# Reordering the first stage of a fused decoder-layer kernel: norm sums ahead of and around the conditioning matmuls

## The reference, cut to what matters

```python
ada = jax.nn.silu(c) @ w_ada + b_ada
sh1, sc1, g1, shm, scm, gm, sh2, sc2, g2 = [a[:, None, :] for a in jnp.split(ada, N_ADA, axis=-1)]
h = modulate(rms_norm(x, ln1), sh1, sc1)
x = x + 0.5 * g1 * swiglu(h, w_f1_up, w_f1_down)
h = modulate(rms_norm(x, ln_mix), shm, scm)
...
x = x + gm * mix
h = modulate(rms_norm(x, ln2), sh2, sc2)
x = x + 0.5 * g2 * swiglu(h, w_f2_up, w_f2_down)
```

## Time and profile before

| | before |
|---|---|
| median of 3 runs | 2063.03 us |
| the profiled execution: its own time | 2063.94 us |
| its span (first to last instruction) | 2062.0 us |
| TensorE busy | 1956.5 us (95%) |
| VectorE / ScalarE / GpSimd busy | 1183.1 / 800.5 / 342.9 us |
| mean granted TensorE clock | 0.975 of full |
| first stage, up to the first `half_shift` | 58.90 us |
| start of the unbroken up matmuls | 92.86 us |

### The profile page before, as it was taken

How to read it: one execution, slowest core, us unless ns; L and a number is a source line. 1 busy time by engine, 2 the same in 40 slices (tenths; PEclk the granted TensorE clock), 3 DMA queues, 4 the chain that set the end, 5 groups by cost and what they waited for, 6 DMA issues and landing times.

```text
span 2062.0 us, 35562 instructions
## 1 busy us (share of the span) xinstructions
PE 1956.5 (95%) x13771; PEld 1887.8 (92%) x13771; DVE 1183.1 (57%) x1880; ACT 800.5 (39%) x1336; POOL 342.9 (17%) x319
## 2 busy tenths in 40 slices
PE   7599999999989999999999989699999999999997
PEld 5499999999979999989899878699999999999997
DVE  4865555555545354656756667755555555555554
ACT  3622232323234234355546554523222232444443
POOL 0222121222100001012103132312222121000000
PEclk9799999999999999999999999899999999999998
DMA  7022222222388675443343423122222222574743
GB/s 275 21 90 76 74 73 83 73 83 73 105 312 293 229 268 205 134 135 99 99 111 98 115 80 98 32 84 73 83 67 76 75 73 63 183 218 137 228 146 121
DMA packets 277621, 255.80 MB, mean 124 GB/s; under 512 B 11202, under 2 KB 222649, under 8 KB 277513
## 3 DMA queue, kind: packets, MB, share of 16 engines
q1 hardware_dynamic: 277357, 254.35, 38.8%
q10 hardware_dynamic: 164, 0.09, 0.0%
HBM read 224.08 MB, written 30.42 MB: 123 GB/s over the span
## 4 chain that ended last, share of the span: by engine, by line
PE 84%; DVE 7%; ACT 4%; DMA 2%; issue 2%; POOL 1%; SPq 0%; DVEq 0%; ACTq 0%; POOLq 0%
PE banks L631 44%; PE banks L667 24%; PE banks L576 9%; PE banks L582 1%; DVE mwl L1429 1%; PE banks L603 1%; DMA araw<-hidden 1%; ACT mwh L1157 1%; DVE y L390 1%; PE banks L587 1%; DVE xo L1434 0%; ACT xo L985 0%; PE banks L823 0%; DVE xT L1531 0%; PE banks L818 0%
## 5 line engine op out<-in xcount | busy, mean ns | idle before, releaser
L631 PE MATMUL banks<-xo,woh 128*128 128x272 f32 x4928 | 944.8, 291 | 38.0 <-DVE xo L1434 19.5
L631 PEld LDWEIGHTS banks<-xo,woh 128*128 128x128 f32 x4928 | 784.0, 191 | 40.5 <-issue 20.6
L631 PE MATMUL banks<-xo,wol 128*128 128x272 f32 x2464 | 718.5, 292 | 0.0
L667 PE MATMUL banks<-ahl,woh 128*128 128x384 f32 (+1 forms) x2112 | 518.7, 329 | 11.6 <-DVE wol L1591 11.4
L631 PEld LDWEIGHTS banks<-xo,wol 128*128 128x128 f32 x2464 | 469.2, 190 | 0.0
L667 PEld LDWEIGHTS banks<-ahl,woh 128*128 128x128 f32 x2112 | 371.6, 189 | 25.5 <-DVE wol L1591 14.8
L667 PE MATMUL banks<-ahl,wol 128*128 128x384 f32 (+1 forms) x1056 | 345.1, 327 | 0.0
L1450 DVE TENSOR_TENSOR pp<-pp,banks 128x544 f32<-128x544 f32 x220 | 154.7, 720 | 214.7 <-PE banks L631 214.7
L1591 DVE TENSOR_TENSOR wol<-ws,woh 128x512 fp32r<-128x512 f32 x264 | 183.3, 698 | 139.0 <-ACT woh L1102 137.9
L1102 ACT ACTIVATE woh<-ws 128x512 fp32r<-128x512 f32 x264 | 164.0, 624 | 166.9 <-PE banks L667 148.5
L576 PE MATMUL banks<-hh,mwh 128*128 128x384 f32 (+1 forms) x600 | 208.6, 348 | 15.3 <-DVE mwl L1429 11.3
(11 more groups left out here) (206 smaller groups left out, 1808.2 us busy)
## 6 DMA issues: line engine op xcount, KB each, us to landing
ws<-in_w_ffn_down SPq DMA_DIRECT2D x264, 256.0 KB, 3.3
ws<-in_w_ffn_up SPq DMA_DIRECT2D x88, 512.0 KB, 4.6
aiD<-in_w_ada SPq DMA_DIRECT2D x14, 2048.0 KB, 8.9
ws<-in_w_in SPq DMA_DIRECT2D x51, 512.0 KB, 3.8
hidden<-post SPq DMA_DIRECT2D x88, 272.0 KB, 2.6
araw<-hidden SPq DMA_DIRECT2D x88, 192.0 KB, 3.9
ws<-in_w_out SPq DMA_DIRECT2D x24, 512.0 KB, 3.7
ai<-in_w_ada SPq DMA_DIRECT2D x4, 2048.0 KB, 20.8
```

The source lines that it names most:

```text
L631: mm = pe.matmul(out, w[:, s, P * k:P * (k + 1)], x_operand(h, j, x)[:, k, :], start=(k == 0 and a == 0), stop=(k == 3 and a == 2))
L667: mm = pe.matmul(ps[4 * (p % 2) + m][:, 0:n], l[:, down_slot(s), P * m:P * (m + 1)], ahl[:, k, x, 0:n], start=(k == 0 and a == 0), stop=(k ...
```

## The change

On TensorE the wait for `csT` (`s_cs` at 2) goes from ahead of the square sums of half 0 to behind them, and the square sums of half 1 are cut in two, with the select of unit 0 between the parts. On ScalarE logarithm and exponential of half 0 come together ahead of those of half 1. On VectorE the slices of `half_scale` are spread in pairs between the unit's copies and stores, and `norm_factor(1)` goes from behind the copy of unit 1 to behind the store of unit 2.

```diff
@@ TensorE @@
-            pe.wait_ge(s_cs, 2)
             pe.wait_ge(s_ones, 1)
             pe.wait_ge(s_trev, 2 * NX)
-
             square_sums(0, 0, KT)
+            pe.wait_ge(s_cs, 2)
+
             for u in range(AU_FIRST):
                 if u == 1:
-                    square_sums(1, 0, KT)
+                    square_sums(1, 0, 4)
                 if u:
                     pe.wait_ge(s_aevc, u)
                     if u >= 2:
                         pe.wait_ge(s_ada, u - 1)
                     ada_select(ps[0], aev0)
+                if u == 1:
+                    square_sums(1, 4, KT)
                 pe.wait_ge(s_ai[u], 16)
                 for k in range(KT):
                     ada_rows(ps[6 + u % 2], k, first_ada(u)[:, k, :]).then_inc(s_apc, 1)
@@ ScalarE @@
-            norm_log(0)
-            norm_log(1)
-            norm_exp(0)
-            norm_exp(1)
+            norm_rsqrt(0)
+            norm_rsqrt(1)
             act.wait_ge(s_cf, 1)
@@ VectorE @@
             ada_sums_of(0)
             norm_factor(0)
+            half_scale(0, 0, 2)
             ada_store_of(0)
+            half_scale(0, 2, 4)
             ada_sums_of(1)
-            norm_factor(1)
-            half_scale(0, 0, 4)
+            half_scale(0, 4, 6)
             ada_store_of(1)
             ada_sums_of(2)
-            half_scale(0, 4, KT)
+            half_scale(0, 6, KT)
             ada_store_of(2)
+            norm_factor(1)
             ada_sums_of(3)
-            half_scale(1, 0, 4)
+            half_scale(1, 0, 2)
             ada_store_of(3)
             dve.wait_ge(s_ada, 4)
             norm_coef(0, 1, R_LN1)
-            half_scale(1, 4, KT)
+            half_scale(1, 2, KT)
```

## The result

The changed kernel takes 2056.05 us, median of 7 runs (2052.82 to 2057.88); in the same number of runs the kernel before takes 2063.03 (2062.42 to 2065.89). The profiled execution took 2055.82 with a span of 2053.9, 8.1 less than the span before.

What follows compares the result with a forecast made beforehand. TensorE is 95% busy, but the prologue ahead of 92.9 us adds its whole length; first shift at 50.6 instead of 58.90, 8.3 us earlier. 2063.03 - 8.3 = 2054.7 us, range 2051.9 to 2057.5.

Steps and rivals of the forecast that it cites:

- TensorE's chain from 17.85 to rows of unit 2: First stage: half 0's sums start at 17.85, take 7.54 us at full clock; rows of unit 2 end at 41.31.
- ScalarE and VectorE ahead of copy 2: First stage: both keep up with TensorE; 3.8 us of VectorE slack cover half of half 0's scaling.
- GpSimd's stretch: VectorE's last pair of half 0's scalings: lengthened once by GpSimd's second operation, 0.96 us; bounds none and two.
- The select of unit 3: TensorE, behind a 3.0 us idle gap: takes 1.88 us, ending at 50.05; at full clock VectorE's pair decides.
- the first rival: First stage: GpSimd's second operation misses the pair and clock holds for select 3; gain 10.1, 2053.0 us; 15%.
- the slower rival: TensorE's first-stage chain, 22.5 us of work, runs at half clock throughout; 14.2 us lost, 2077; 2%.
- Behind `coef`: After `coef`: six instead of four scalings of half 1, 3.9 us, covered by VectorE's wait for ScalarE; price 0.
- The later stretch: Unbroken matmuls, which start with 5.5 us at clock 0.50: where that ends may shift, 1 us either way.
- C: Distance from the start of the unbroken matmuls to the end of the span; 1969.1 us before, 1970.5 changed.
- The clock in half 0's sums: Rival: the clock falls there all the same, 9.29 instead of 7.54 us, all on the chain; 2056.5 us; 11%.
- A: Distance from the end of the last transposes to the start of rows of unit 0; 11.17 us before, 7.69 changed.
- B: Distance from the start of rows of unit 0 to the first shift; 30.01 us before, 23.99 changed.

Runs made afterwards that it cites:

- e6: Changed kernel with GpSimd's first combination held until `coef` is written; 2058.77 us (1 run), kernel before in the same set 2061.62.
- e7: Changed kernel with TensorE's wait for `csT` back ahead of half 0's square sums; 2056.30 us (1 run), kernel before in the same set 2061.62.
- the second set: The changed kernel run once more, nothing altered, and profiled again; median 2053.73 us (5 runs), kernel before in the same set 2065.39.
- e1: Kernel before with only TensorE's wait for `csT` moved behind half 0's square sums; 2060.49 us (1 run), kernel before in the same set 2060.67.
- e11: Changed kernel with half 1's square sums in four pairs, factor 1 split around `coef`, 16 identity transposes while x arrives; 2051.02 us, ratio 0.9934.

## Why the prediction was right, step by step

- **TensorE's chain from 17.85 to rows of unit 2** came as worked out: start 17.85, rows 0 at 25.4, rows 1 at 35.6, the end of rows 2 at 41.4 against 41.31. This is addition of durations from the trace of before.
- **ScalarE and VectorE ahead of copy 2** had the slack claimed: VectorE waited 3.96 for rows 1 and 1.74 for rows 2, and the added table loads were hidden.
- **GpSimd's stretch** was taken as 0.96 and was 0.59 (1.94 less 1.35), measured again by taking it away (e6). It started on the second operation at 41.57 and took 1.26, so 0.72 of it was left when the pair began at 42.11; the sum had 0.86 left of it (to 43.0, from 42.14) and charged 0.96. Its place was right.
- **The select of unit 3** is the step that was wrong: "I take 1.88, the nearer case". It took 1.06 behind a gap of 2.55; VectorE's pair decided, as in the alternative of the same paragraph. In one execution the clock did fall there: in e7 the select took 1.63 behind a gap of 1.96. So the step was a guess between two cases, not a wrong chain. With the smaller stretch this makes the first shift 49.34 instead of 50.6, in the direction of the first rival.
- **TensorE's gaps**: the slower rival was played down with "no idle gap over 0.8 us before 41 us"; the walk itself has one of 0.97 ahead of the select of unit 1 (37.43 to 38.40), and 0.89 was measured. It changed nothing, the clock stayed at 1.00.
- **Behind `coef`** the price of 0 was 0.13 (34.09 less 33.96).
- **The later stretch** was allowed 1 us either way, near its start. In fact C moved by 1.3 in the profile and by up to 7 between kernels, in instructions far behind. That is where the error of the method lies.
- **The clock in half 0's sums** was the rival with 11%. It fell in 5 of 8 profiled executions with the wait behind. Where it fell, A was 9.7 on average instead of 7.7: 2.0 us, about the 1.75 given. The chance was much too small, because I took the idle gap of 1.9 us as the sole cause. The profiles give 6.0 from B and from A 3.5 if the clock holds, 1.5 if it falls, so 7.5 to 9.5 with C's scatter on top. The profiled execution, with a gain of 8.1, fits this. For the medians, 7.0 in the first set and 11.7 in the second, it is only an account, as nobody saw the clock or C in the runs that were not profiled.

The time was forecast at 2054.7 and is 2056.05, in the range. The mechanism of the stage was right: the chain, its handover to VectorE and GpSimd's place came as worked out. That the number came so close is partly luck, as errors of opposite sign met: in the profile the stage was 1.3 better and the rest 1.4 worse than forecast, and the second set came 1.0 below the forecast where the first came 1.4 above.

## What to carry to other kernels

When two engines hand work back and forth, order their lists together: each of the two reorderings by itself gave 0.9 or cost 2.5, and the pair gave 6.0 (one profile for each variant, two for the pair). What must come first on the waited-for engine is whatever lets the other go on (the copies), and everything else goes into the time it waits. Compare such variants by distances within the trace, not by the time of the whole, when the rest scatters by more than the effect.

## What the runs showed of the hardware that was not expected

- TensorE's granted clock fell to 0.50 while TensorE was at work: in e1 it was down from 18 us on, in the middle of the transposes, 1.8 us after the end of a gap of 1.42 (ahead of x's eighth tile).
- It also held through a gap of 2.55 us ahead of the select of unit 3 (and of 2.59 in the second profile), but fell behind 1.96 ahead of the square sums in the kernel before, and during the select of unit 3 behind 1.96 in e7. The length of the gap alone does not tell.
- The same instructions from the first unbroken matmul to the end took 1964.5 to 1971.5 us in fourteen profiles; that is 0.36% of the time, more than any single part of this change is worth. In e6 and e11, 6.3 us apart, TensorE was busy for the same time within 0.3 us; the rest is idle time.
- A VectorE operation with two inputs in SBUF that begins beside a GpSimd operation is shown as longer, not as waiting: in the kernel before two of them took 1.68 and 1.67 where others of the kind take 0.72, and each ended 0.59 and 0.58 behind GpSimd's operation. In the change a pair took 1.94, and 1.35 with GpSimd held back (e6).
